# A hybrid decoder step on one core: the sample's cache pages issued in another order on SyncE's queue

## What is computed

```python
k_past = cache_k[l][page_table].reshape(DEC_BATCH, n_pages * PAGE_SIZE, H_A, 2, DQK)
v_past = cache_v[l][page_table].reshape(DEC_BATCH, n_pages * PAGE_SIZE, H_A, DV)
a_s = diff_attention(qs, k_all, v_all, ...)     # k_all: past and own keys
s_s = s5_mixer(us, ...)                         # state space part
x1 = layer_norm(ALPHA * x + concat(a_s, s_s) @ w_out)
y  = layer_norm(ALPHA * x1 + peer_apply(x1))    # 8 heads x 16 retrieved experts a row
```

## Time and profile before

| | us |
|---|---|
| median of 3 runs | 3775.09 (3774.56 to 3777.10) |
| profiled execution | 3767.13 |
| its span in the profile | 3765.3 |
| TensorE busy | 2626.8 |
| VectorE busy | 2436.2 |
| ScalarE busy | 1511.6 |
| GpSimd busy | 1286.1 |

### The profile page before, as it was taken

How to read it: one execution, slowest core, us unless ns; L and a number is a source line. 1 busy time by engine, 2 the same in 40 slices (tenths; PEclk the granted TensorE clock), 3 DMA queues, 4 the chain that set the end, 5 groups by cost and what they waited for, 6 DMA issues and landing times.

```text
span 3765.3 us, 44267 instructions
## 1 busy us (share of the span) xinstructions
PE 2626.8 (70%) x14060; PEld 1104.1 (29%) x14060; DVE 2436.2 (65%) x5648; ACT 1511.6 (40%) x4363; POOL 1286.1 (34%) x1099
## 2 busy tenths in 40 slices
PE   7877778876677667766776677577766776557755
PEld 4565444331123112311231233123312332222311
DVE  8603755488558755975596669665966696335775
ACT  1103324344444344434443544453445344334433
POOL 0000233334543444344334443444344333113334
PEclk9868889887787678768876788678868776778866
DMA  5342889999999999999999999999999999788988
GB/s 140 79 129 89 327 295 377 388 406 377 419 382 396 387 403 374 397 382 417 375 386 390 413 378 382 400 412 377 373 399 411 370 370 395 287 300 332 403 328 340
DMA packets 241576, 1316.27 MB, mean 350 GB/s; under 512 B 41682, under 2 KB 69106, under 8 KB 91058
## 3 DMA queue, kind: packets, MB, share of 16 engines
q0 software_dynamic: 156672, 1140.92, 75.6%
q1 hardware_dynamic: 78784, 163.78, 12.5%
q10 hardware_dynamic: 5890, 8.75, 0.7%
HBM read 1293.78 MB, written 17.97 MB: 348 GB/s over the span
## 4 chain that ended last, share of the span: by engine, by line
DVE 30%; DMA 27%; PE 24%; ACT 7%; issue 7%; SPq 3%; POOL 2%; DVEq 0%; POOLq 0%; ACTq 0%
DMA UV<-in_peer_uv,zone_x 24%; DVE zone_z L1514 12%; PE psum L1172 9%; PE psum L1094 3%; PE psum L472 3%; DMA wq<-in_cache_k 2%; DVE zone_x L1416 2%; DVE zone_x L1419 2%; DVE zone_x L1417 2%; PE psum L337 2%; POOL UV L987 2%; PE psum L1114 2%; DVE zone_x L1418 1%; ACT D L1282 1%; DVE zone_z L1478 1%
## 5 line engine op out<-in xcount | busy, mean ns | idle before, releaser
L1172 PE MATMUL psum<-UV,D 64*64 64x512 f32 x8704 | 1516.1, 790 | 921.9 <-ACT D L1282 892.9
L987 POOL DMA_INDIRECT UV<-in_peer_uv,zone_x x1088 | 1280.7, 1177 | 2375.3 <-PE psum L1172 1915.6
L1514 DVE CUSTOM_DVE_ANT_0 zone_z<-UV,zone_x 128x1024 bf16<-128x1024 f32 x1088 | 1333.7, 1226 | 776.4 <-DMA UV<-in_peer_uv,zone_x 703.4
L1277 ACT ACTIVATE ge<-acts 128x1 f32<-128x1 f32 x1088 | 219.7, 202 | 1662.4 <-DVE acts L1514 1658.3
L1172 PEld LDWEIGHTS psum<-UV,D 64*64 64x64 f32 x8704 | 314.8, 160 | 1805.7 <-issue 1769.3
L1282 ACT ACTIVATE D<-id,wge 128x64 f32<-128x64 f32 x1088 | 378.3, 348 | 35.4
L1279 ACT ACTIVATE wge<-ge,zone_x 128x1 f32<-128x1 f32 x1088 | 320.5, 295 | 35.3
L1114 PE MATMUL psum<-wq,zone_z 128*128 128x256 f32 (+1 forms) x1152 | 306.1, 425 | 1.2 <-ACT zone_z L1223 1.2
L1114 PEld LDWEIGHTS psum<-wq,zone_z 128*128 128x128 f32 (+1 forms) x1152 | 234.5, 209 | 117.4 <-issue 69.9
L1277 ACT ACT_TABLE_LOAD x113 | 145.0, 1283 | 2.8 <-ACT vrows L584 0.8
L1094 PE MATMUL psum<-w_out_sb,zone_z 128*128 128x512 f32 (+1 forms) x256 | 116.0, 607 | 0.0
(11 more groups left out here) (280 smaller groups left out, 2331.6 us busy)
## 6 DMA issues: line engine op xcount, KB each, us to landing
wq<-in_peer_w_q SPq DMA_DIRECT2D x72, 1024.0 KB, 8.3
UV<-in_peer_uv,zone_x POOLq DMA_INDIRECT x1088, 9.9
wq<-in_cache_k SPq DMA_DIRECT2D x64, 256.0 KB, 8.9
vrows<-in_cache_v SPq DMA_DIRECT2D x64, 256.0 KB, 9.0
wq<-in_w_in SPq DMA_DIRECT2D x10, 1024.0 KB, 6.4
zone_x<-in_x_all SPq DMA_DIRECT2D x9, 512.0 KB, 8.1
UV<-in_w_out SPq DMA_DIRECT2D x1, 4096.0 KB, 22.2
w_out_sb<-in_w_out SPq DMA_DIRECT2D x1, 4096.0 KB, 32.8
```

What stands on the lines that cost most here:

```text
L987: pool.indirect_dma_start(out=UV[:, n % RING, :], out_offset=None, in_=table, in_offset=bass.IndirectOffsetOnAxis(ap=icur[:, t % 2, column ...
L1172: ins = pe.matmul(bank[6 + r][q:q + 64, :], D[64 * r:64 * r + 64, n % RING, :], UV[64 * r:64 * r + 64, n % RING, DM + 512 * e:DM + 512 * e ...
L1277: act.activation(ge[:, j:j + 1], acts[:, j:j + 1], ACT.Gelu).then_inc(sem("gelu_done"), 1)
L1514: dve.tensor_tensor_reduce(out=junk[:, :], in0=UV[:, n % RING, 0:DM], in1=x1[:, t % 2, :], scale=1.0, scalar=0.0, op0=ALU.mult, op1=ALU.ad ...
```

## The change

Within `sp_front`, for tile 8 only. For batches 1 to 6 the wait and the issues for the first half of the next keys stand ahead of the wait for `s_O`, and the second half stays behind the values. For batch 0 the order is what it was.

```diff
                 for b in range(DB):
 
+                    if 0 < b < DB - 1:
+                        wait(sp, "s_KTps", 8 * b + 4)
+                        sp_pages(sp, b + 1, "k", 0)
                     wait(sp, "s_O", b)
                     sp_pages(sp, b, "v", 0)
                     sp_pages(sp, b, "v", 1)
                     if b == 0:
                         wait(sp, "topk_done", EH * NT)
                     sp.dma_start(vnew, vrows[DS * b:DS * b + DS, NT, :]).then_inc(sem("vnew_in"), 16)
+                    if b == 0:
+                        wait(sp, "s_KTps", 4)
+                        sp_pages(sp, 1, "k", 0)
                     if b < DB - 1:
-                        for half in range(2):
-
-                            wait(sp, "s_KTps", 8 * b + 4 * half + 4)
-                            sp_pages(sp, b + 1, "k", half)
+                        wait(sp, "s_KTps", 8 * b + 8)
+                        sp_pages(sp, b + 1, "k", 1)
```

## The result

The changed kernel takes 3719.4 us in the median of 4 runs (3713.9 to 3726.1), beside 3776.1 before: a ratio of 0.9846 with a 95% interval of 0.9833 to 0.9859, 56.7 us less. Measured twice more, it gave 0.9848 (0.9814 to 0.9882) and 0.9858 (0.9835 to 0.9882). The forecast was 3730 us in a range of 3712 to 3750.

What follows compares the result with a forecast made beforehand. A chain of waits through SyncE's issues bound six rounds of 217.8 us; at 27.9 us each by bytes, 50.4 us won, less 5 for refilling gather buffers, net 45: from 3775.1 to 3730 us, range 3712 to 3750.

Steps and rivals of the forecast that it cites:

- The binding chain: Six 36.3 us rounds, batches 1 to 7, limited by waits through SyncE's issues, not engines or transfers; six waits at stake.
- The slower outcome: Rival: value pages land behind gathers, moved keys in 33.6 us; rounds of 43.4 us, about 3818 us; chance 0.04.
- the null: Rival: first half of the keys isn't released before the values end, so nothing changes; 3775 us; chance 0.03.
- The margin: SyncE finishes the four moved key issues and is back 1.6 us before the values end, so value pages aren't held back.
- What is late next: Four candidates for the new round length: compute, value pages, second half of keys, bytes; bytes largest at 27.9 us.
- the compute candidate: Round length if the engines' work bounds it: 3248.07 to TensorE's last work at 3269.04, 21.0 us.
- The sum: Six rounds: 217.8 - 6 x 27.9 = 50.4 us won, less 5 for refilling gather buffers, net 45 us.
- the term of the bytes: Six rounds move 65.49 MB, 10.9 MB a round, at 391 GB/s: 27.9 us a round.
- the debt: Gathers stocked in six buffers during the old waits must be fetched later: 0 to 10.7 us, taken as 5.
- The partial case: Rival: value pages take 20.5 us to land behind gathers; rounds of 30.3 us, 3744 us; chance 0.20.
- The rate of 357 GB/s: Rival: transfers in the six rounds hold only 357 GB/s, 183.4 us for them; 3746 us; chance 0.08.
- four prices in a row: Old round, batch 3 to 4: work until values end 11.9, value issues 9.8, key issues 4.9, landing 8.5; sum 35.1 us.

Runs made afterwards that it cites:

- the first trace: Profiled execution of the changed kernel from its first measurement: median 3719.4 us, ratio 0.9846 to before; its six rounds took 159.2 us.
- the third trace: The changed kernel unaltered, measured and profiled once more beside a follow-up version: 3714.0 us, ratio 0.9858 to before; six rounds 169.3 us.
- the second trace: The changed kernel unaltered, measured and profiled again beside follow-up versions: 3714.6 us, ratio 0.9848 to before; six rounds 151.9 us.

## Why the prediction was right, and where it was off

**The binding chain** was right in place and in number: six waits of some 14 us, behind SyncE's issues, and all six went. The slower outcome and the null did not come. SyncE is back in time, as worked out: in the changed kernel it waits for the values for 18.2 us in six rounds, 3 us each, so the moved issues never held the value pages back. (The margin had been worked out with 4.4 us for the four issues, where the chain in the earlier trace rows has 4.9: 1.2 us and not 1.6.)

**What is late next** was right in the main: the DMA engines are full (a share of 1.01), with the second half of the keys close behind. The predicted rate was 391 GB/s, the measured one 388 in the first trace. But one sign did not come: the expert loop does not wait for gathers there, as it does elsewhere. The full engines show as late pages instead. And the compute candidate was put too low, at 21.0 us: it ended with TensorE's last work ahead of the long wait and left out the 3.9 us for a diagonal that this wait had hidden. The chain is 24.1 us from the second round on. As the bytes were still longer, the forecast did not suffer by it.

The pattern said of the second half (its reader stands behind the values, so that a wait only delays the round after) is in the starts of the rounds: 20.9, 30.9, 24.1, 30.6, 24.1, 28.7 us. The lengths alternate in the first and the third trace, and hardly in the second. Its waits in the first are these, the third pair of key transposes in the three long rounds:

```profile
3223.56 1.09 PE L1038 MATMUL psum<-ident,wq 128*128 128x128 f32 x8 [1.79 <-DMA wq<-in_cache_k]
...
3278.23 1.09 PE L1038 MATMUL psum<-ident,wq 128*128 128x128 f32 x8 [1.49 <-DMA wq<-in_cache_k]
...
3331.19 1.97 PE L1038 MATMUL psum<-ident,wq 128*128 128x128 f32 x8 [3.13 <-DMA wq<-in_cache_k]
```

**The sum was too small, 45 us against 56.7.** The step that failed is the term of the bytes. I took the 65.49 MB that the old six rounds moved, and took 5 us off for the debt in gather buffers as well. But the old rounds moved so much because they filled those buffers; with the stock smaller, 62.17 MB pass in the rounds and the rest passes after them. 3.32 MB at 388 GB/s is 8.6 us. For the 2.35 MB of gathers in it, 6.1 us, the debt was counted twice; the 1.0 MB of key pages, 2.5 us, was counted into rounds behind which it lands. The debt alone was well sized: the last stretch took 36.7 us where it took 33.2, and 40.0 and 38.2 in the other two traces, 3.5 to 6.8 us for the 5 that I took. With 62.17 MB at 391 GB/s the rounds come to 159.0 us, where 159.2 were measured, and the gain to 58.8 - 5 = 54. That this meets the first trace to 0.2 us is in part luck: the second trace has 151.9 and the third 169.3 us with as many bytes within 1 MB. By the whole stretch (rounds and last) the three traces gained 55.0, 59.1 and 43.5 us, so a single trace would not have told the forecast's 45 from the 56.7 of the medians.

**The two profiled executions** differ by 48.2 us in their spans, less than the medians do and less than the 55.0 us of the stretch, because the changed one came to batch 1's keys 6.5 us later, behind a part where both programs are the same (the last section has the rows).

**The rivals.** The partial case (pages behind the gathers) did not set the rounds here, but the two kernels that start the value pages later show it to be near: rounds of 30.4 and 31.3 us, beside its 30.3. The rate of 357 GB/s did not come as a limit; the third trace has 363 over its rounds, at a share of 0.96, with the DMA engines full in its waits for pages (1.03 in the two longest) and thinner behind them. The Trainium skill's "DMA: Bandwidth & Descriptors", section Specifications, would have capped the rounds at about 358 GB/s; the rows with 388 and 403 GB/s over 150 us and more disagree with it. The same page's rule on turns between queue rows (section Queues, rings and completion order) was not isolated by any run here.

**What was right for a reason that doesn't hold** is the reading of the chain as four prices in a row, 11.9 + 9.8 + 4.9 + 8.5. Its sum fits the round to a tenth of a microsecond, as a chain from the trace must, yet shortening the second term by 3.8 us brought 1.6. The last term took up most of the difference.

## What to carry to other kernels

When a wait ends with a transfer's landing, ask what else the queue held. If the DMA engines were full up to the landing, the time from issue to landing may be the rest of a backlog, and grow by most of what an earlier issue saves (here 2.4 us in the median of 3.8). Then look for what stands ahead of the awaited transfer in its queue without being needed sooner: that order alone was worth 35 us here. And look for the stretch in which the queue was thin, with a buffer free by then: issuing there was worth 21 us more. The worth of such a move is not the time of its own bytes (2.7 us for the 1.05 MB of a group, where each moved group won 9.8). It is the time in which the DMA engines had little to do, and it ends at whichever comes next, the bytes of a round or the engines' own chain. Every transfer that the move pushes back must still have slack of its own: the two versions that pushed the value pages back gave 21 and some 33 us away.

And when stalls had filled a ring of buffers, don't charge the refill twice. Either count the bytes of the steady state, or count the old bytes and no debt. And when a long wait goes, look for shorter waits of other engines that it had hidden, before calling the rest of the round its compute.

## What the runs showed that was not expected

- A faster issue of the same transfers is largely paid back in landing: 3.8 us saved by SyncE in a round, 2.4 us more to land in the median of the key pages (8.4 to 10.8).
- The same program's rounds lay between 151.9 and 169.3 us in three traces, at 403 and 363 GB/s at the ends, with the same instructions. The spread of its times, 3707.8 to 3726.6 in 15 of 16 executions, is of that size. One took 3679.3 us, and one of the kernel before 3747.6; neither has a trace, and their cause is open.
- Two executions of the same part of the program were 6.8 us apart, by the load of tile 7's input rows on SyncE's timeline, of before and of the changed kernel:

```profile
2717.70 0.33 SPq L929 DMA_DIRECT2D zone_x<-in_x_all  x1
```

```profile
2724.52 0.33 SPq L933 DMA_DIRECT2D zone_x<-in_x_all  x1
```

A difference of two profiles has that much noise here.
